# Moved statistics, splits and loads at four block seams of a 36,000-instruction fp32 kernel

## The reference

```
def _rms(x, gain):
    y = xf * rsqrt(mean(xf * xf, axis=-1) + EPS)
    return y * gain
def _swiglu(h, w_in, w_out):
    gate, up = split(h @ w_in, 2); return (silu(gate) * up) @ w_out
# dilated: q = rms(h @ w_q) * q_gain * d ** -0.5; s = q k^T + bias; softmax; o = p v; o @ w_o
```

## Time and profile before

| | us |
|---|---|
| median of 3 runs | 1957.86 |
| lowest, highest | 1954.37, 1959.96 |
| profiled execution, its own time | 1954.76 |
| its span | 1952.7 |
| TensorE busy in it | 1894.5 |
| VectorE, ScalarE, GpSimd busy | 1195.3, 976.6, 112.6 |

### The profile page before, as it was taken

How to read it: one execution, slowest core, us unless ns; L and a number is a source line. 1 busy time by engine, 2 the same in 40 slices (tenths; PEclk the granted TensorE clock), 3 DMA queues, 4 the chain that set the end, 5 groups by cost and what they waited for, 6 DMA issues and landing times.

```text
span 1952.7 us, 36124 instructions
## 1 busy us (share of the span) xinstructions
PE 1894.5 (97%) x15516; PEld 1811.5 (93%) x15516; DVE 1195.3 (61%) x1387; ACT 976.6 (50%) x1139; POOL 112.6 (6%) x52
## 2 busy tenths in 40 slices
PE   7999999899999989999999999999999998999999
PEld 7879999898999989999999999888999987779999
DVE  7667766655866775558667555533555566647554
ACT  7365444545544454345446343776634456655332
POOL 0000000110000000000000000333000011220000
PEclk9999999999999999999999999999999999999999
DMA  7315454443554445555335554455555546425552
GB/s 272 123 56 187 177 189 155 154 146 104 180 190 168 177 140 204 178 172 176 124 112 194 175 191 172 158 173 174 183 184 181 185 162 178 113 95 194 189 176 104
DMA packets 57977, 320.53 MB, mean 164 GB/s; under 512 B 6144, under 2 KB 19536, under 8 KB 20752
## 3 DMA queue, kind: packets, MB, share of 16 engines
q1 hardware_dynamic: 55968, 314.76, 47.1%
q10 hardware_dynamic: 1904, 4.24, 0.6%
HBM read 317.85 MB, written 1.12 MB: 163 GB/s over the span
## 4 chain that ended last, share of the span: by engine, by line
PE 87%; DVE 7%; ACT 3%; issue 2%; DMA 1%; SPq 0%; DVEq 0%; ACTq 0%
PE bank L396 27%; PE bank L398 26%; PE bank L397 26%; DVE lo L346 2%; ACT hi L340 1%; PE bank L463 1%; PE bank L1905 1%; PE bank L500 1%; PE bank L2256 1%; DVE xl L970 1%; PE bank L481 0%; DMA ring<-in_dq 0%; DVE arena L556 0%; PE bank L1298 0%; DVE x L980 0%
## 5 line engine op out<-in xcount | busy, mean ns | idle before, releaser
L396 PE MATMUL bank<-xh,hi 128*128 128x256 f32 x2960 | 846.9, 286 | 17.5 <-DVE lo L369 9.9
L397 PE MATMUL bank<-xl,hi 128*128 128x256 f32 x2960 | 839.4, 284 | 0.0
L398 PE MATMUL bank<-xh,lo 128*128 128x256 f32 x2960 | 839.2, 283 | 0.0
L346 DVE TENSOR_TENSOR lo<-ring,hi 128x2048 fp32r<-128x2048 f32 x274 | 623.6, 2280 | 304.4 <-ACT hi L340 304.1
L340 ACT ACTIVATE hi<-ring 128x2048 fp32r<-128x2048 f32 x290 | 549.2, 1898 | 418.5 <-PE bank L398 407.4
L396 PEld LDWEIGHTS bank<-xh,hi 128*128 128x128 f32 x2960 | 568.2, 192 | 26.4 <-issue 16.2
L397 PEld LDWEIGHTS bank<-xl,hi 128*128 128x128 f32 x2960 | 568.3, 192 | 2.3 <-issue 1.5
L398 PEld LDWEIGHTS bank<-xh,lo 128*128 128x128 f32 x2960 | 568.2, 192 | 0.5
L396 PE MATMUL bank<-gh,hi 128*128 128x256 f32 x1056 | 300.3, 284 | 9.3 <-DVE gl L900 9.3
L398 PE MATMUL bank<-gh,lo 128*128 128x256 f32 x1056 | 299.3, 283 | 0.0
L397 PE MATMUL bank<-gl,hi 128*128 128x256 f32 x1056 | 299.3, 283 | 0.0
(11 more groups left out here) (256 smaller groups left out, 1863.2 us busy)
## 6 DMA issues: line engine op xcount, KB each, us to landing
ring<-in_ffn_in SPq DMA_DIRECT2D x132, 1024.0 KB, 4.9
ring<-in_ffn_out SPq DMA_DIRECT2D x66, 1024.0 KB, 4.9
ring<-in_kv SPq DMA_DIRECT2D x24, 1024.0 KB, 4.9
ring<-in_hg_in SPq DMA_DIRECT2D x16, 1024.0 KB, 4.8
ring<-in_od_in SPq DMA_DIRECT2D x12, 1024.0 KB, 4.8
ring<-in_dq SPq DMA_DIRECT2D x12, 1024.0 KB, 4.9
ring<-in_ev_in SPq DMA_DIRECT2D x10, 1024.0 KB, 5.1
arena<-rel_rows SPq DMA_DIRECT2D x24, 256.0 KB, 3.6
```

Of the source, the lines that this page charges most:

```text
L346: ns.tensor_tensor(lo[n % RING][:, 0:w], ring[n % RING][:, 0:w], hi[n % RING][:, 0:w].bitcast(F32), ALU.subtract).then_inc(lo_ok[lo_by[n]], 1)
L396: nc.tensor.matmul(out_, lh, rh, start=start, stop=False, **kw)
L397: nc.tensor.matmul(out_, lh, rl, start=False, stop=False, **kw)
L398: return nc.tensor.matmul(out_, ll, rh, start=False, stop=stop, **kw)
```

## The change

Six edits. (1) In dilated VectorE takes the low part of chunk 3 instead of GpSimd. (2) In `ff_in` a hook `between` is called after the first 24 matmuls of a step; in glu0 `pe_final_stats` is put there. (3) In conv0 the last step splits the low part of fox's chunk 1 too. (4) In kv `pe_stats` is moved from ahead of chunk 1 into its middle. (5) In dilated the six bias loads are issued after the load of chunk 5. (6) In dilated `QG` stands behind the four evictions.

```diff
             elif b == "dilated":
-                lo_by += ["P" if c == 3 else "V" for c in range(len(streams[b]))]
+                lo_by += ["V" for c in range(len(streams[b]))]
...
-        def ff_in(pe, j, par, n, F, first, it=None):
+        def ff_in(pe, j, par, n, F, first, it=None, between=None):
...
                 for e in range(2):
+                    if between is not None and h == 0 and e == 1:
+                        between(pe)
...
-            ff_in(pe, 1, 1, n + 2, F, None)
-            if b == FINAL:
-                pe_final_stats(pe)
+            ff_in(pe, 1, 1, n + 2, F, None, None, pe_final_stats if b == FINAL else None)
...
             elif not first:
-                lo_until(dve, m + (5 if par else 4))
+                lo_until(dve, m + (5 if par or b == "conv0" else 4))
...
                     if value:
-                        pe_wide(pe, n0 + c, value_banks(k // 2), k % 2, k % 2 == 0, c == 23, mean if early else None)
+                        pe_wide(pe, n0 + c, value_banks(k // 2), k % 2, k % 2 == 0, c == 23,
+                                mean if early else lambda: pe_stats(pe, "kv"))
...
-                    if c == 0:
-                        pe_stats(pe, "kv")
...
-                for p in {4: [0], 8: [1], 10: [2], 12: [3], 13: [4], 15: [5, 6, 7]}.get(c, []):
+                for p in {5: [0], 8: [1], 10: [2], 12: [3], 13: [4], 15: [5, 6, 7]}.get(c, []):
...
             def dve_part(dve):
+                for c in range(4):
+                    take_out(dve, c)
                 nc.vector.tensor_scalar(QG[:, :], vecs[:, ROW_QG:ROW_QG + 3], DH ** -0.5, None, ALU.mult).then_inc(qg_ok, 1)
                 dve.wait_ge(qg_ok, 1)
-                for c in range(4):
-                    take_out(dve, c)
```

## The result

| | before | after |
|---|---|---|
| median of 4 runs, side by side, us | 1957.3 | 1940.47 |
| lowest, highest | 1954.37, 1959.96 | 1939.39, 1942.38 |
| profiled execution | 1954.76 | 1939.39 |
| its span | 1952.7 | 1937.2 |

The ratio is 0.992, with a 95% interval of 0.9901 to 0.9938: 16.8 us faster in the medians, 15.4 in the profiled executions. The forecast was 1937.

A forecast was written before the change was run, and what follows sets the result against it. TensorE, busy 97% of the span, was taken as the bound, with its waits and slow-clock time to win. 5.0 + 8.6 + 1.8 + 5.4 = 20.8 us off gave a median of 1937 us, range 1930 to 1946.

The forecast's parts named there:

- The sign: Whole kernel: faster at 0.94, same at 0.03, slower at 0.03.
- the largest term: glu0: final statistic issued inside input step 1, no wait before output step 0; gain 8.6 us, ends 7.2 and 9.
- the term of kv: kv: statistics moved into chunk 1 let `mean` start earlier; gain 1.8 us, ends 0.9 and 3.1.
- dilated: dilated: scores start 3.0 us earlier, fast clock gives 2.2 more, plus 0.2; gain 5.4 us, ends 3.0 and 7.
- conv0 to fox: Start of fox: TensorE no longer waits for chunk 1's low part; gain 5.0 us, ends 4.5 and 6.0.
- the first rival: Clock falls after the new waits in fox (1.5 us) and kv (1.6): 1940 us, chance 0.22.
- `mean` can start at 1239.95: kv: `mean` starts at 1239.95 and not 1241.83, 1.8 us earlier, after a new wait of 1.2 us.
- Edits 1 and 6: 0 us: dilated: moving GpSimd's low part to VectorE and `QG` behind the evictions gains 0 us, ends -0.5 and +0.5.
- take-over of the relay: Another wait takes over in fox and dilated, through ScalarE's packed queue: 1942 to 1943 us, chance 0.15.
- long stretch of low clock: TensorE without pauses is granted the low clock for long, as over a third of dilated: 1967 us, chance 0.03.
- up to one microsecond: dilated: freeing VectorE's low parts from SBUF contention with GpSimd would give up to a microsecond more, outside the sum.

The follow-up runs named there:

- the repaired kernels: Changed kernel with kv's constants issued ahead of ScalarE's wait for the statistics (1936.43 us), or with SP holding back weight chunk 5's load until they land (1937.22 us).
- the filling: Changed kernel with 12 products of dilated's chunk 5 between the first groups of scores and chunk 7's high part taken early: 1941.58 us, ratio 0.9919.
- GpSimd back: Changed kernel with GpSimd taking the low part of dilated's chunk 3 again: 1941.33 us, ratio 0.9911.

## Why the prediction was right, and where it failed

The sign, the range of 1930 to 1946 and the size of the largest term held; the term of kv came out with the wrong sign. The sum was 20.8 us, the profile gives 15.5. The 5.3 us between them are kv 3.36, fox 1.23, dilated 0.44 and the start 0.32.

*conv0 to fox.* The mechanism was right: the products stand right behind conv0 at 354.35, and the wait at the gate grew from 1.03 to 1.64 us (forecast 1.9). `rs_b` came 4.69 us earlier after the cut (forecast 4.5), and TensorE passed the gate 5.26 us earlier. Without a clock fall the stretch takes 322.86, a gain of 5.30 against the forecast's 5.0. That is seen in the kernel with the constants moved, whose fox code is the same; its TensorE row and its windows:

```profile
381.15 0.39 PE L396 MATMUL bank<-xh,hi 128*128 128x256 f32 x1 [1.65 <-DVE cum_r L1792]
```

```profile
376.00:380.00 4.00, 3.50 (x26) 2.96 (x25) 3.18 (x4) 4.00 (x4) 0.40 (x1) 1.00 0.00 0
380.00:384.00 4.00, 2.85 (x23) 2.85 (x24) 2.66 (x4) 2.30 (x3) 4.00 (x1) 1.00 0.75 248
```

In six of eight profiles the clock falls after this wait (0.64 in the window shown of after), and 1.5 us go. So this term is 3.8 or 5.3, and the first rival, priced at 1.5 us here, was right about it.

*glu0.* All as forecast: L692 inside step 1, at 693.40, no wait ahead of output step 0, 0.27 us ahead of input step 2 (0.5), 8.63 us (8.6). It held because each engine's part of the relay was read off rows, with slack on both sides. That it came out to the second digit is in part luck: in three other profiles with the code of before this stretch is 0.2 to 0.5 us longer.

*kv: this step failed, twice.* First, "`mean` can start at 1239.95": it can't, because it also waits for `consts`. That load was not in the working at all. Before, it landed 1.8 us after its issue at 1234.84 and hid behind the chain of squares. In ScalarE's program it stands behind the wait for the statistics; when these moved, its issue moved too, onto SP's next load. That cost 2.0 us, the difference of 44.36 and 42.36. Second, the base: the earlier trace rows is one execution with a clock fall that five kernels with the same kv code did not repeat. The forecast's chain, 1.88 us earlier than 44.20, gives 42.32 for L2256, and the repaired kernels have 42.36; but without the edit and without the fall it is 42.60. The true worth was 0.2 us. The chain itself was read rightly: the squares ended 42.21 us after the cut, and the forecast has them at 42.3.

*dilated.* The scores right behind chunk 4: 3.05 us (forecast 3.0). Two groups of scores at 0.92 us, the third in part slow; in a kernel without a fall all three are fast, and chunk 5's products start 5.23 us earlier than before, as in the forecast's 3.0 + 2.2 + 0.2. In the profile after, the fall behind the 0.8 us waits takes 0.66 of it back. How near 4.96 is to 5.4 is in part luck: six profiles with all three edits and without the filling range from 288.28 to 289.73, by where the clock falls. Wrong was "Edits 1 and 6: 0 us" as a statement on the edits: it is true of them only on top of edit 5. Alone, moving `QG` starts the scores 3.05 us earlier, since the first eviction comes 2.44 us earlier and not 0 to 0.5. That edit 5 carries the gain, as the forecast has it, is true, but the gain is capped by chunk 4's end, so either repair gets all of it.

*The rivals.* The time of the first, 1940, is what was measured, but only half of its mechanism: in fox the clock fell as it said; in kv it fell behind a wait of 3.22 us that no rival named. A take-over of the relay did happen in kv, by a transfer, where the forecast looked for it in fox and dilated. No long stretch of low clock came; the mean granted clock is 0.997.

*The rule of the Trainium skill* weighed for GpSimd ("GPSIMD Engine Reference", section 1, Specifications: shared access to SBUF, contention for two-input instructions on VectorE) is seen at work in these runs: in fox a low part on VectorE took 3.50, 4.23 and 4.95 us and ended about 2.15 us after GpSimd's each time. The forecast's up to one microsecond from it in dilated did not come. There no low part on VectorE was slowed in the kernel before (each took 2.28 or 2.29 us); the one that overlaps GpSimd's had begun first, and GpSimd's took 5.94 us, where most of its low parts take 4.6. The scores start at 43.39 with GpSimd's part or without.

Open is what decides whether the clock falls after one and the same wait. It was not settled, only counted: after the fox wait of 1.64 or 1.65 us it fell in both profiles of the changed kernel and in four others with the same fox code, and stayed up in two (constants moved; GpSimd back).

## What to carry to other kernels

When a step is moved earlier, list everything that its release lets go on each engine behind it, transfers included, and look at what each queue issues at that moment. Price a gain at one clock on both sides: a low stretch in one profile is luck until a second execution shows it. When two edits repair one chain, test each alone, for one of them may be enough.

## What the runs showed of the hardware

A 64 KB load took 1.8 us from issue to landing when it was issued 1.09 us ahead of the next 1 MB load of another queue or when that load was held back, 5.7 to 6.2 us in five profiles where it was issued within 0.02 us of one, and 3.9 and 4.1 us when issued 1.05 us after one.

A `tensor_scalar` of three columns on VectorE took 2.41 us beside a low part of GpSimd, ending within 0.02 us of it (1583.61 and 1583.59), and 0.16 without. A low part on VectorE that began during GpSimd's ended about 2.15 us after it, whether 2.8, 2.1 or 1.4 us of GpSimd's were left when it began. So in these rows the later one waited until the earlier was done, and the time that it is recorded with is mostly the wait. Evictions and the reciprocal on VectorE ran beside the same GpSimd instruction at their usual 0.69 and 1.75 us.

After a wait of 1.41 us in kv the granted clock fell in one profile and stayed up in five; after 1.64 or 1.65 us in fox it fell in six and stayed up in two; after 2.9 to 3.4 us in kv it fell in three and stayed up in two. The first two cost 1.6 and 1.5 us where it fell.
